# A three-stage block in float32: the opening's ACT order, the first mixer norm, the mixer's block inputs, output halves and last pooling rearranged

## The reference

```python
# first block, twice
proj = x @ w_in                       # queries, keys, values, gates
ya = neighbourhood_attention(...)     # 8 heads
yb = bidirectional_retention(...)     # 4 heads, decay tables from sigmoid(ret_decay)
merged = sigmoid(gate_a) * (ya @ w_branch_a) + sigmoid(gate_b) * (yb @ w_branch_b)
x = layer_norm(ALPHA * x + merged @ w_out)
x = layer_norm(ALPHA * x + conv_glu_ffn(x) + sigmoid(x @ w_ple_gate) * (p @ w_ple_proj))
# second block, once ("the mixer")
u = rmsnorm(h) @ w_in_2               # 512 channels to pooling, 512 to the SSM
y_pool = ((trailing mean over 2, 4, 8, 16 positions - u_pool) @ w_pool) * pool_scale
y_ssm = ssm(u_ssm); y_ssm = gelu(y_ssm); y_ssm = y_ssm * sigmoid(y_ssm @ w_glu + b_glu)
h = h + concat(y_pool, y_ssm) @ w_out_2
h = h + swiglu(rmsnorm(h)); return rmsnorm(h)
```

## Time and profile before

| what | value |
|---|---|
| median of three runs | 2319.66 us (2319.19 to 2320.61) |
| profiled execution | 2319.28 us, span 2317.4 us |
| TensorE busy | 2287.2 us, 11672 matmuls |
| VectorE, ScalarE, GpSimd busy | 962.9, 973.4, 1149.2 us |
| mean granted clock of TensorE | 0.997 of full speed |
| moved by DMA | 214.18 MB, 92 GB/s over the span |

### The profile page before, as it was taken

The page is one execution under the profiler, slowest core; times in us unless marked ns, Lnnn a source line. Parts: engine busy times, 40 slices in busy tenths (PEclk is TensorE's granted clock), DMA queues, the critical chain, the costliest instruction groups (busy, mean ns, idle before and its releaser), DMA issues.

```text
span 2317.4 us, 32473 instructions
## 1 busy us (share of the span) xinstructions
PE 2287.2 (99%) x11672; PEld 1890.9 (82%) x11672; DVE 962.9 (42%) x1611; ACT 973.4 (42%) x1372; POOL 1149.2 (50%) x702
## 2 busy tenths in 40 slices
PE   8999999999999999999999999999999999999998
PEld 7888888888888887888888888888888777888886
DVE  6355343344444204453553353334376774222201
ACT  5444443244555325444453243555512534443321
POOL 3433334578995455333334465444455666444452
PEclk9999999999999999999999999999999999999999
DMA  5222223322223422222222323233333213233321
GB/s 208 77 67 88 79 80 101 100 85 93 91 93 106 135 92 84 70 88 79 78 83 91 100 83 100 91 100 100 100 103 107 65 38 109 91 100 100 99 92 55
DMA packets 61284, 214.18 MB, mean 92 GB/s; under 512 B 7200, under 2 KB 7456, under 8 KB 61216
## 3 DMA queue, kind: packets, MB, share of 16 engines
q1 hardware_dynamic: 58336, 205.10, 27.9%
q10 hardware_dynamic: 2880, 8.15, 1.1%
HBM read 211.13 MB, written 2.10 MB: 92 GB/s over the span
## 4 chain that ended last, share of the span: by engine, by line
PE 94%; DVE 3%; POOL 1%; ACT 1%; issue 1%; DMA 0%; DVEq 0%; ACTq 0%
PE psum L825 85%; PE psum L853 2%; PE psum L854 2%; PE psum L858 2%; PE psum L956 1%; PE psum L944 1%; PE psum L923 1%; POOL run L774 1%; PE psum L1223 0%; DVE states L2241 0%; PE psum L1012 0%; PE psum L1049 0%; DVE pr L1886 0%; POOL run L780 0%; POOL u_all L783 0%
## 5 line engine op out<-in xcount | busy, mean ns | idle before, releaser
L459 POOL TENSOR_TENSOR w_lo<-stage,w_hi 128x1024 fp32r<-128x1024 f32 x378 | 926.3, 2459 | 1070.7 <-ACT w_hi L1369 1055.8
L825 PE MATMUL psum<-xh,w_hi 128*128 128x512 f32 x1712 | 671.2, 392 | 0.7 <-DVE scaled L2366 0.7
L825 PE MATMUL psum<-xl,w_hi 128*128 128x512 f32 x1712 | 666.9, 390 | 0.0
L825 PE MATMUL psum<-xh,w_lo 128*128 128x512 f32 x1712 | 666.4, 389 | 0.0
L1369 ACT ACTIVATE w_hi<-stage 128x1024 fp32r<-128x1024 f32 x377 | 396.4, 1052 | 379.1 <-PE psum L825 377.6
L825 PEld LDWEIGHTS psum<-xh,w_hi 128*128 128x128 f32 x1712 | 321.3, 188 | 71.9 <-issue 2.4
L825 PEld LDWEIGHTS psum<-xh,w_lo 128*128 128x128 f32 x1712 | 321.4, 188 | 67.3
L825 PEld LDWEIGHTS psum<-xl,w_hi 128*128 128x128 f32 x1712 | 321.5, 188 | 65.0
L825 PE MATMUL psum<-g_hi,w_hi 128*128 128x512 f32 x528 | 206.2, 391 | 0.0
L825 PE MATMUL psum<-g_hi,w_lo 128*128 128x512 f32 x528 | 205.4, 389 | 0.0
L825 PE MATMUL psum<-g_lo,w_hi 128*128 128x512 f32 x528 | 205.4, 389 | 0.0
(11 more groups left out here) (399 smaller groups left out, 3359.3 us busy)
## 6 DMA issues: line engine op xcount, KB each, us to landing
stage<-in_w SPq DMA_DIRECT2D x379, 512.0 KB, 3.5
bias_raw<-in_bias ACTq DMA_DIRECT2D x8, 384.0 KB, 3.0
z<-in_x SPq DMA_DIRECT2D x3, 512.0 KB, 8.0
out_x<-out_t SPq DMA_DIRECT2D x3, 512.0 KB, 2.7
p_raw<-in_p ACTq DMA_DIRECT2D x2, 512.0 KB, 3.4
masks_raw<-in_masks SPq DMA_DIRECT2D x1, 576.0 KB, 11.1
masks_raw<-in_masks ACTq DMA_DIRECT2D x1, 576.0 KB, 4.6
z<-in_x SPq DMA_DIRECT2D x2, 256.0 KB, 5.5
```

Of the source, the lines that this page charges most:

```text
L459: pool.tensor_tensor(w_lo[s][:, :, :], stage[s][:, :, :], w_hi[s][:, :, :].bitcast(F32), ALU.subtract).then_inc(lo_done, 1)
L825: mm = pe.matmul(dst, lhs[i], rhs[j], start=start and n == 0, stop=stop and n == 2)
```

## The change

Six edits, none of which changes a value that is computed.

1. ACT's opening: `first_high(0)` comes before the decay steps, and the Ln step after the x tiles.
2. First mixer norm: three tiles of unit 3 (nine matmuls) come before the spread and five after it. ACT copies one part of the convolution kernel before the root in place of the second pair of `b_apart`, and the rest of both before it rounds units 4 and 5.
3. `block_inputs(1)` comes before `convolve(0)`.
4. The first output unit (`first_halves`) runs the high passes of both halves tile by tile, the low passes of half 0 one tile behind, and those of half 1 at the end.
5. GpSimd's last pooling comes after the low part of unit 13 (`MS_U0 + 3`), and `pool_product(3)` after unit 13 in place of after unit 12. DVE's program is not changed.
6. The second norm's spread comes at step 8 in place of step 9.

```diff
             pool.wait_ge(state_im, SP_T)
-            for g in range(SP_T):
+            for g in range(SP_T - 1):
                 pooling(g)
-                mixer_low(10 + g)
-            for u in range(10 + SP_T, GU_U0):
+                mixer_low(MS_U0 + g)
+            mixer_low(MS_U0 + SP_T - 1)
+            pooling(SP_T - 1)
+            for u in range(MP_U0, GU_U0):
                 mixer_low(u)
...
+                def in_part(m, dst, tiles):
+                    for k in tiles:
+                        mm = passes(dst[:, :], wt(MIN_U0 + m, k), xm_parts(k), k == 0, k == KT - 1)
+                    return mm
...
+                def first_halves(u0, r0, ready, parts):
+
+                    def low_half(h, k):
+                        pe.wait_ge(*ready(k))
+                        return low_pass(U_BANK[(r0 + h) % 2][:, :], wt(u0, 4 * h + k), parts(k), k == SP_T - 1)
+
+                    for k in range(SP_T):
+                        pe.wait_ge(mix_hi_s, k + 1)
+                        for h in range(2):
+                            if k == 0:
+                                take_bank(MIX, r0 + h)
+                            high_passes(U_BANK[(r0 + h) % 2][:, :], wt(u0, 4 * h + k), parts(k), k == 0)
+                        if k:
+                            low_half(0, k - 1)
+                    low_half(0, SP_T - 1).then_inc(mid_done, 1)
+                    for k in range(SP_T):
+                        mm = low_half(1, k)
+                    mm.then_inc(unit_used, 1)
...
-                        order = [(h, k) for h in range(2) for k in range(SP_T)]
                         if together and u == 0:
-                            order = [(h, k) for h in range(2) for k in range(SP_T - 1)] + [(h, SP_T - 1) for h in range(2)]
+                            first_halves(u0, r0, ready, parts)
...
                 variance(n0, sq_1)
+                take_unit(MIX, MIN_U0 + 3)
+                in_part(3, O_BANK, range(3))
                 spread(n0, rstd_1)
-                in_unit(3, O_BANK)
+                in_part(3, O_BANK, range(3, KT)).then_inc(unit_used, 1)
                 pe.wait_ge(wb_apart, 2 * BT)
                 pe.wait_ge(kernel_ready, 4)
                 block_inputs(0)
                 in_unit(4, take_bank(MIX, MIN_R0 + 4))
+                block_inputs(1)
                 convolve(0)
-                block_inputs(1)
                 in_unit(5, take_bank(MIX, MIN_R0 + 5))
...
-                    for g in ((), (2,), (3,), ())[i]:
+                    for g in ((), (2,), (), (3,))[i]:
                         pool_product(g)
...
-                    if k == KT + 1:
+                    if k == KT:
                         spread(n0 + 1, rstd_2)
...
-                b_apart(BT - 1)
-                b_apart(BT - 2)
-                root(n0, rstd_1, (square_mean, 1))
-                ahead(1)
-                ahead(2)
-                for j in range(BT - 3, -1, -1):
-                    b_apart(j)
-                act.wait_ge(kernel_done, SP_T)
-                for h in range(4):
+                def kernel_apart(h):
+                    act.wait_ge(kernel_done, SP_T)
...
+                b_apart(BT - 1)
+                kernel_apart(0)
+                root(n0, rstd_1, (square_mean, 1))
+                for h in range(1, 4):
+                    kernel_apart(h)
+                for j in range(BT - 2, -1, -1):
+                    b_apart(j)
+                ahead(1)
+                ahead(2)
                 ahead(3)
                 ahead(4)
...
+            first_high(0)
             act.wait_ge(decay_in, 16)
             flat = decay[:, :, :].rearrange("p d n -> p (d n)")
             act.activation(decay_a[:, :], flat, ACT.Abs).then_inc(decay_step, 1)
             act.wait_ge(decay_step, 1)
             act.activation(decay_a[:, :], decay_a[:, :], ACT.Exp, scale=-1.0).then_inc(decay_step, 1)
-            act.wait_ge(decay_step, 2)
-            act.activation(decay_a[:, :], decay_a[:, :], ACT.Ln, bias=1.0).then_inc(decay_step, 1)
-            first_high(0)
             for k in range(KT):
...
                 if k == 1:
                     first_high(1)
+            act.wait_ge(decay_step, 2)
+            act.activation(decay_a[:, :], decay_a[:, :], ACT.Ln, bias=1.0).then_inc(decay_step, 1)
             first_high(2)
```

More of the change, by code:

```diff
@@ L1204, in xm_parts @@
                     return xm_hi[:, k, :], xm_lo[:, k, :]
+                def in_part(m, dst, tiles):
+                    for k in tiles:
+                        mm = passes(dst[:, :], wt(MIN_U0 + m, k), xm_parts(k), k == 0, k == KT - 1)
+                    return mm
                 def in_unit(m, dst):
                     take_unit(MIX, MIN_U0 + m)
-                    for k in range(KT):
-                        mm = passes(dst[:, :], wt(MIN_U0 + m, k), xm_parts(k), k == 0, k == KT - 1)
-                    mm.then_inc(unit_used, 1)
+                    in_part(m, dst, range(KT)).then_inc(unit_used, 1)
                 def block_inputs(q):
@@ L1264, in half_units @@
                         take_unit(MIX, u0 + u)
-                        order = [(h, k) for h in range(2) for k in range(SP_T)]
                         if together and u == 0:
-                            order = [(h, k) for h in range(2) for k in range(SP_T - 1)] + [(h, SP_T - 1) for h in range(2)]
-                        for h, k in order:
-                            if k == 0:
+                            first_halves(u0, r0, ready, parts)
+                        else:
+                            for h in range(2):
                                 take_bank(MIX, r0 + 2 * u + h)
-                            pe.wait_ge(*ready(k))
-                            mm = passes(U_BANK[(r0 + h) % 2][:, :], wt(u0 + u, 4 * h + k), parts(k), k == 0, k == SP_T - 1)
-                            if k == SP_T - 1:
+                                for k in range(SP_T):
+                                    pe.wait_ge(*ready(k))
+                                    mm = passes(U_BANK[(r0 + h) % 2][:, :], wt(u0 + u, 4 * h + k), parts(k), k == 0, k == SP_T - 1)
                                 mm.then_inc(unit_used if h else mid_done, 1)
```

## The result

| what | before | after |
|---|---|---|
| median of 12 runs each | 2319.76 us (2318.88 to 2320.61) | 2325.98 us (2323.55 to 2327.64) |
| span of the profiled execution | 2317.4 us | 2324.6 us |
| VectorE, GpSimd busy | 962.9, 1149.2 us | 972.9, 1144.2 us |
| mean granted clock of TensorE | 0.997 | 0.996 |

The changed kernel is slower: 6.2 us by the medians, a ratio of 1.0028 with a 95% interval of 1.002 to 1.0036. The forecast was 1.5 us faster, and the time lies 5.5 us above the end of its range.

A forecast was written before the change was run, and what follows sets the result against it. TensorE was taken as the path nearly everywhere, so edits count by its waits. Terms -1.2 - 1.8 - 0.3 - 0.8 - 0.5 + 3.1 = -1.5 us gave 2318.1 us from 2319.66, with an 8-in-10 range of 2316.0 to 2320.5.

The forecast's parts named there:

- Opening: Kernel's start: first matmul 2.1 us earlier, but DVE's held decay-table operation caps the gain at 1.3; 1.2 us gained.
- the forecast's other sentence: Opening: if the clock's rise stays at 13.8, three more products fit before it, worth 0.9 us in all.
- the rival's 1.4 us: Opening: DVE's hold does not appear and the clock rises early, 1.4 us more gained, 2316.7 us; chance 0.10.
- Fourth unit around the spread: First mixer norm: nine matmuls put first cover TensorE's 1.9 us reciprocal wait; 1.8 us gained, bounds 1.4 and 2.0.
- cover 0.6 us: After the first norm: ACT's copies end at 1825.1, TensorE arrives for block inputs 0 at 1825.7.
- cover 0.7 us: After block inputs 0: unit 4's low part is ready at 1828.8 and needed at 1829.5.
- Block inputs 1 ahead of convolve 0: Mixer states: DVE's 1.4 us wait goes, pooling starts some 3 us earlier; 0 for TensorE unless pooling's lateness counts.
- Halves: First output unit: four matmuls behind the first half shorten the bank wait; 0.3 us gained, 0.1 to 0.4.
- Second spread: Second norm: spread one step earlier removes the next unit's 0.7 us wait for `scaled`; 0.8 us gained, 0.6 to 0.9.
- Last pooling: Around unit 13: 0.5 us wait goes, but DVE's queue holds the bank TensorE needs; 3.1 us lost, 2.9 to 3.8.
- the clock falls in the new stall: Rival behind the last pooling product: TensorE's clock drops, likelier cost 1.6 us, so 2319.7 us; chance 0.27.
- slower by over 0.2%: Whole kernel above 2324.3 us, expected only from something unseen or a very long low clock; chance 0.03.

The follow-up runs named there:

- run 2: Kernel before with only the first norm's change: unit 3 split round the spread, ACT's copies before the rounding of units 4 and 5; 2322.69 us, 1.0014.
- Run 4: Changed kernel with ACT's rounding of units 4 and 5 put back right behind the root; 2320.42 us, 1.0006 of the kernel before.
- run 7: Kernel before, with GpSimd alone waiting for block inputs 0 before the low parts of units 5 to 7; 2325.04 us, 1.0025.
- run 6: Kernel before with only the first output unit's halves skewed and the second norm's spread one step earlier; 2318.78 us, 0.9997.
- Run 3: Changed kernel with DVE's ssm_half(6) and ssm_half(7) put ahead of mix_low(3); 2321.78 us, 1.001 of the kernel before.
- run 1: Kernel before with only the last pooling moved behind unit 13's low part and pool_product(3) behind unit 13; 2324.16 us, 1.0019.
- run 5: Kernel before with only the opening changed: unit 0 rounded before the decay steps; 2318.30 us, 0.9994.
- run 8: Changed kernel with the pooling move undone, three kernel copies before the root and units 4 and 5 rounded right behind it; 2316.15 us, 0.9985.
- run 9: Changed kernel, pooling still moved: three kernel copies, root, rounding of units 4 and 5; DVE's ssm_half(6) and ssm_half(7) ahead of mix_low(3); 2317.13 us, 0.999.

## Why the prediction was wrong

**Bound.** Right: TensorE sets the end nearly everywhere, and the whole difference is in its waits and its clock.

**Opening.** Forecast 1.2 us gained, capped by a held decay-table operation. The size is right: 1.1 us by its own run (an interval that holds 0), 1.06 at unit 2 in the changed kernel, of which 0.73 was left at the mixer. The cap is right for the changed kernel, where unit 2 waits for it. In the edit's own run it does not bind: the clock rose at 13.7 there, and three more products before the rise gave 0.9 us, as the forecast's other sentence had it. That the two came out within 0.2 us of each other was luck. The rise at "near 10.3", on which the rival's 1.4 us rested, is shown by no row: the earliest in these profiles is 12.1, in the changed kernel, and it brought next to nothing.

**Fourth unit around the spread: the step that failed.** The forecast "1.8 us gained, bounds 1.4 and 2.0" is right up to block inputs 0, 1.97 us. But it priced the moved roundings of units 4 and 5 as "cover 0.6 us" and "cover 0.7 us", the time until TensorE needs unit 4. That it did not wait for unit 4 is right. What the step left out is that the low parts of units 4 to 8 move with the roundings, onto DVE's state tiles, and that DVE is held there, though the opening's own cap was worked out from just this kind of hold. In the forecast's terms, the price of late low parts was put at nothing as long as TensorE did not wait for the unit itself. It cost 4.7 us by the table, and run 2 turned the whole edit from -1.8 into +3.3. Run 4 took it back, and run 7 made it without the edit.

**Block inputs 1 ahead of convolve 0.** Forecast 0, "unless pooling's lateness counts". Its own run gives 0.5 us less, not told from 0, but in its profile the lateness does count: 0.67 us less between product 3 and unit 13. "Pooling starts some 3 us earlier" was too large: it was 0.9 in that run, since DVE kept one wait of 0.64 us and its later tiles were already back to back. In the changed kernel pooling started 4.6 us later than before (1878.79, was 1874.19): the first state tile alone took 15.1 us in place of 9.7.

**Halves.** Forecast 0.3, measured 0.35 in the stretch. The sum took it as kept; run 6 shows that it isn't where unit 13's low part follows the last pooling.

**Second spread.** Forecast 0.8, measured 0.81 (from mean square to the next unit, 7.23 to 6.42 us).

**Last pooling.** Mechanism right, and the size within its bounds. Forecast +3.1 and -0.5: the wait came to 4.40 us of distance less the product's 0.9, 3.5 (bounds 2.9 and 3.8), mostly since `mix_lo`, which starts beside a row of low parts that ends at 1926.16, took 1.2 us, to the addition's start, in place of 0.84; and what went at the old place is 0.4 (1913.34 to 1914.62, less 0.9). Net +3.1 in place of +2.6. Run 3 shows the order as the cause. A term was missing: edit 5 also puts two low parts in a row under `mix_low(0)` and `mix_low(1)`, which hold up `ssm_half(2)` behind them. With the late states of edit 2 this cost 1.2 us at product 2.

**The clock.** The rival "the clock falls in the new stall", chance 0.27 and priced 1.6 us, came true in the changed kernel's profile at 1.3 us, and in run 1's at some 2.6. Near this length the outcome differed from profile to profile: stalls of 3.4 us (after) and 3.24 us (run 1) were followed by the lower level, one of 3.19 us (run 4) was not.
The Trainium skill (TensorE: Matmul & The Clock Gate, section Why this matters for your kernels) asks for no such gap; the trace agrees for two of the three, and has falls behind shorter waits too, of 2.90 us (the changed kernel, block inputs 3) and of 1.9.
The fall at the mixer's entry showed in the profiles of the changed kernel and of runs 4 and 6, and not in the nine others, the kernel before among them, with the same 1.9 us wait. I do not know what decides it; in the changed kernel's profile it is 1.4 us that the medians need not carry in full, and it may be part of why the spans differ by 7.2 and the medians by 6.2.

**Sum.** With what was measured, stretch by stretch: -0.7 (opening, as kept at the mixer) + 1.4 (clock at its entry) - 2.0 + 4.7 (block inputs and states) - 0.35 (halves) + 1.2 (product 2) + 3.1 (product 3) + 1.3 (clock) - 0.8 (second spread) - 0.5 (clock, in the last spread) = +7.3, beside the spans' +7.2. The chance given to "slower by over 0.2%", 0.03, was far too low. The rivals were all single places on TensorE's own path, and no case asked what the moved work does to another engine while it runs.

## What to carry to other kernels

A weight's low part that is "moved to where nobody needs it yet" still occupies GpSimd, and while it ran here it held VectorE's additions, subtractions and scans on SBUF. So for each moved piece, besides who waits for its result, read which VectorE operations lie under its new place, and whether TensorE waits for those. When a product is moved on TensorE, move its consumers in every in-order queue with it, or the release that TensorE needs next stands behind them. Measure edits of a few microseconds one at a time: here two of six turned the sign of the whole, and with one of them undone and the other's roundings put back early the kernel was 3.3 us faster than before.

## What the runs showed of the hardware

- VectorE beside GpSimd's 128x1024 subtraction: a 128x512 addition of two SBUF operands took 1.65 and 2.88 us in place of 0.68, two subtractions of 0.69 each 4.32 in all, eight 128x128 scans 4.76 and 6.95 in place of 2.63, a 128x896 `TENSOR_SCALAR` 2.82 where its like took 0.69. Operations with an operand in PSUM kept 0.68. In these rows the engine that was under way kept its time: a subtraction that started amid VectorE's row took 5.20 us in place of 2.4, and the row's operations kept their 0.69.
The Trainium skill (SBUF — State Buffer, section SBUF: two separate sides) says that the two engines share a port pair under an exclusive lock, held for a whole instruction by whichever starts first. The rows agree, both ways (2.88 us for 0.68 on VectorE, 5.20 for 2.4 on GpSimd).
- The granted clock after a stall is not a function of its length alone in these profiles. Behind pool product 3 it was at the lower level after 3.38 and 3.24 us and full after 3.19, yet it also fell behind a wait of 2.90 us at block inputs 3; and at the mixer's entry, with one and the same 1.9 us wait, three profiles of twelve show the lower level, for 3.4 us each.
- Matmuls left the slow pace at 12.1 us in the changed kernel and at 13.7 in run 5, whose opening has the same order and whose first matmul starts 0.1 us apart (6.89 and 6.79). With the old opening it was 13.8 in the kernel before and 12.4 in run 2 (first matmuls at 9.18 and 9.00).
- Near 903 us, behind thin work on TensorE, one profile (the changed kernel) has no fall of the clock and eleven have one. In runs 2, 3, 8 and 9 it lasted twice as long as in the others, and TensorE lost 1.2 to 1.3 us there against the kernel before. A difference of a microsecond between two single profiles is thus no measure of an edit; the runs' medians, or one stretch at a time, are.
